# A two-layer hybrid decoder trunk on one core: the gate rows of the attention scores spread over 128 partitions, and another order of work where a residual stage closes

## The reference

```python
c_act = silu(c)
for i in range(2):
    mod = c_act @ ada_w[i] + ada_b[i]
    sh_mix, sc_mix, g_mix, sh_mlp, sc_mlp, g_mlp = split(mod, 6)
    h = rmsnorm(x, norm_mix[i]) * (1 + sc_mix) + sh_mix
    mix = fox_mixer(h) if i == 0 else short_conv_mixer(h)
    x = x + g_mix * mix
    h = rmsnorm(x, norm_mlp[i]) * (1 + sc_mlp) + sh_mlp
    x = x + g_mlp * (square(relu(h @ w_up)) @ w_down)
return rmsnorm(x, final_norm)
```

```python
s = q_t @ k_s * scale + F[t] - F[s]      # s <= t only
```

## Time and profile before

| | before |
|---|---|
| median of 3 runs | 2396.4 us (2382.73 to 2397.29) |
| the profiled execution's own time | 2394.39 us |
| its span, first to last instruction | 2392.7 us |
| mean granted clock of TensorE | 0.979 of full |
| PE busy | 2320.2 us, 97% |
| DVE busy | 1630.4 us, 68% |
| ACT busy | 1052.2 us, 44% |
| transfers | 615.61 MB, mean 257 GB/s |

### The profile page before, as it was taken

How to read it: one execution, slowest core, us unless ns; L and a number is a source line. 1 busy time by engine, 2 the same in 40 slices (tenths; PEclk the granted TensorE clock), 3 DMA queues, 4 the chain that set the end, 5 groups by cost and what they waited for, 6 DMA issues and landing times.

```text
span 2392.7 us, 29047 instructions
## 1 busy us (share of the span) xinstructions
PE 2320.2 (97%) x11331; PEld 1952.3 (82%) x11331; DVE 1630.4 (68%) x1539; ACT 1052.2 (44%) x1183; POOL 173.1 (7%) x338
## 2 busy tenths in 40 slices
PE   5999999989999999999998999998999999999998
PEld 5988989768888888888886888876888888888886
DVE  5757877767866766776776888755786455455455
ACT  4344433445434434434444444444543443443443
POOL 0001111100100100100100111100010000000000
PEclk8999999999999999999998999999999999999999
DMA  9978878767977977987984899854896655655563
GB/s 364 387 247 282 310 275 334 269 245 246 313 274 246 314 277 239 323 281 227 324 282 161 312 339 332 310 164 153 280 320 208 194 189 185 191 192 190 190 201 122
DMA packets 270530, 615.61 MB, mean 257 GB/s; under 512 B 14704, under 2 KB 15040, under 8 KB 269504
## 3 DMA queue, kind: packets, MB, share of 16 engines
q1 hardware_dynamic: 220480, 437.29, 53.9%
q0 software_dynamic: 46080, 167.79, 19.7%
q10 hardware_dynamic: 3840, 8.68, 1.0%
HBM read 611.62 MB, written 2.10 MB: 257 GB/s over the span
## 4 chain that ended last, share of the span: by engine, by line
PE 90%; DMA 3%; DVE 3%; ACT 2%; issue 1%; SPq 0%; ACTq 0%; DVEq 0%
PE ps L441 26%; PE ps L443 26%; PE ps L442 26%; DMA start_ring<-in_ada_w_dram 3%; PE ps L428 2%; PE ps L430 2%; PE ps L429 2%; PE ps L720 1%; PE ps L481 1%; PE ps L478 1%; ACT w_hi L790 1%; DVE acc L1198 1%; DVE w_lo L1183 1%; PE ps L640 0%; PE ps L641 0%
## 5 line engine op out<-in xcount | busy, mean ns | idle before, releaser
L1183 DVE TENSOR_TENSOR w_lo<-raw,w_hi 128x1024 fp32r<-128x1024 f32 x740 | 903.8, 1224 | 624.8 <-ACT w_hi L790 622.5
L790 ACT ACTIVATE w_hi<-raw 128x1024 fp32r<-128x1024 f32 x740 | 783.6, 1060 | 1149.1 <-PE ps L443 1060.7
L441 PE MATMUL ps<-w_hi,h 128*128 128x512 f32 x1536 | 610.1, 397 | 6.5 <-DVE h L1296 6.5
L443 PE MATMUL ps<-w_lo,h 128*128 128x512 f32 x1536 | 602.6, 392 | 0.0
L442 PE MATMUL ps<-w_hi,h 128*128 128x512 f32 x1536 | 602.2, 392 | 0.0
L441 PE MATMUL ps<-w_hi,mid 128*128 128x512 f32 x1280 | 503.7, 393 | 2.6 <-DVE mid L1689 2.6
L443 PE MATMUL ps<-w_lo,mid 128*128 128x512 f32 x1280 | 499.6, 390 | 0.0
L442 PE MATMUL ps<-w_hi,mid 128*128 128x512 f32 x1280 | 499.2, 390 | 0.0
L441 PEld LDWEIGHTS ps<-w_hi,h 128*128 128x128 f32 x1536 | 291.4, 190 | 69.0 <-issue 9.3
L443 PEld LDWEIGHTS ps<-w_lo,h 128*128 128x128 f32 x1536 | 291.0, 189 | 62.1
L442 PEld LDWEIGHTS ps<-w_hi,h 128*128 128x128 f32 x1536 | 291.7, 190 | 59.2 <-issue 0.5
(11 more groups left out here) (201 smaller groups left out, 1248.6 us busy)
## 6 DMA issues: line engine op xcount, KB each, us to landing
ada_raw<-in_ada_w_dram POOLq DMA_DIRECT2D x320, 512.0 KB, 6.3
raw<-in_mlp_w_up_dram SPq DMA_DIRECT2D x128, 1024.0 KB, 5.3
raw<-in_mlp_w_down_dram SPq DMA_DIRECT2D x128, 1024.0 KB, 6.4
raw<-in_fox_w_in_dram SPq DMA_DIRECT2D x48, 1024.0 KB, 9.2
raw<-in_conv_w_in_dram SPq DMA_DIRECT2D x48, 1024.0 KB, 7.2
start_ring<-in_ada_w_dram SPq DMA_DIRECT2D x64, 512.0 KB, 11.7
raw<-in_fox_w_out_dram SPq DMA_DIRECT2D x16, 1024.0 KB, 7.7
raw<-in_conv_w_out_dram SPq DMA_DIRECT2D x16, 1024.0 KB, 5.2
```

Source lines behind the costliest of these rows:

```text
L441: mm(o, xh, hi, start=(k == 0), stop=False)
L443: last = mm(o, xh, lo, start=False, stop=(k == KC - 1))
L790: op(w_hi[:, e % WR], raw[:, e // 2, EK * (e % 2):EK * (e % 2 + 1)], ACT.Copy).then_inc(hi_ready, 1)
L1183: v.tensor_tensor(w_lo[:, e % WR], raw[:, e // 2, EK * (e % 2):EK * (e % 2 + 1)], w_hi[:, e % WR].bitcast(F32), ALU.subtract).then_inc(spl ...
```

## The change

Three things are changed.

1. `sel` and `nf` get 128 partitions. `nf` is cleared once by a new memset on GpSimd (so rows 64 to 127 are zero), the matmul of line 640 reads `sel` [128, 1] broadcast to [128, 128] and `nf` [128, n], and every wait on `const_ready` is raised by one. ACT writes `nf[0:64]` and waits for `const_ready` first.
2. In a closing with a norm (not the last one), `stats_block(norm_i, 0)` runs right after block 0 is added, with `split(un.u, 4)` between the reciprocal and the wait for the root; and `split(un.u, 5)` leaves its place ahead of `add_block(.., 1)`.
3. DVE then makes its chunks of `hb` for pairs 0 and 1 one after the other, then the low part of h's pair 0, then `split(un.u, 5)`, then h's low part of pair 1, then `split` 6 and 7. ACT does `norm_pair` 1 ahead of `split(un.u, 7)`.

```diff
-        sel = sb("sel", [4 * H, H], F32R)
+        sel = sb("sel", [P, H], F32R)
-        nf = sb("nf", [4 * H, T], F32R)
+        nf = sb("nf", [P, T], F32R)
@@ gpsimd
+            pool.memset(nf[:, :].bitcast(F32), 0.0).then_inc(const_ready, 1)
-            pool.wait_ge(const_ready, 7)
+            pool.wait_ge(const_ready, 8)
@@ tensor
-            pe.wait_ge(const_ready, 8)
+            pe.wait_ge(const_ready, 9)
-                    pick = sel[:, NB * g + j:NB * g + j + 1].broadcast_to([4 * H, P])
+                    pick = sel[:, NB * g + j:NB * g + j + 1].broadcast_to([P, P])
@@ scalar
+                act.wait_ge(const_ready, 15)
-                op(nf[:, :], ps[0:4 * H, 7, 0:T], ACT.Copy, scale=-1.0).then_inc(f_act, 1)
+                op(nf[0:4 * H, :], ps[0:4 * H, 7, 0:T], ACT.Copy, scale=-1.0).then_inc(f_act, 1)
...
                 split(un.u, 6)
-                if norm_i is not None:
-                    norm_pair(norm_i, 0)
+                norm_pair(norm_i, 0)
+                norm_pair(norm_i, 1)
                 split(un.u, 7)
-                if norm_i is not None:
-                    norm_pair(norm_i, 1)
-                    scale0(norm_i, 2)
-                    norm_pair(norm_i, 2)
+                scale0(norm_i, 2)
+                norm_pair(norm_i, 2)
@@ vector
-            def inverse_rms(a, calls):
+            def inverse_rms(a, calls, between=None):
                 stat(v.reciprocal(recip[:, a], ms[:, a]))
+                if between is not None:
+                    between()
                 dve.wait_ge(root_ready, calls + 1)
...
+                elif norm_i is not None:
+                    stats_block(norm_i, 0, lambda: split(un.u, 4))
                 else:
                     split(un.u, 4)
-                    if norm_i is not None:
-                        stats_block(norm_i, 0)
                     split(un.u, 5)
                 done(un)
                 add_block(un, n, 1, closed)
...
+                stats_block(norm_i, 1)
+                scale1(norm_i, 0)
+                scale1(norm_i, 1)
+                norm_pair(norm_i, 0, False)
+                norm_pair(norm_i, 1, False)
+                low(norm_i, 0)
+                split(un.u, 5)
+                low(norm_i, 1)
                 split(un.u, 6)
                 split(un.u, 7)
-                if norm_i is not None:
-                    scale1(norm_i, 2)
-                    norm_pair(norm_i, 2)
+                scale1(norm_i, 2)
+                norm_pair(norm_i, 2)
```

More of the change, by code:

```diff
@@ L394, in _ @@
             for i in range(2):
-                pool.wait_ge(const_ready, 9 + i)
+                pool.wait_ge(const_ready, 10 + i)
                 pool.affine_select(out=sel[:, :], in_=sel[:, :].bitcast(F32), compare_op=ALU.not_equal, fill=1.0,
@@ L574, in forget_sums @@
                 pe.wait_ge(f_step, 5)
-                pe.wait_ge(const_ready, 14)
+                pe.wait_ge(const_ready, 15)
                 for a in range(TT):
@@ L1002, in residual @@
                         hooks[i]()
-                if norm_i is not None:
-                    act.wait_ge(added0, r0 // NG + 1)
-                    square(norm_i, n, 0)
+                if norm_i is None:
+                    for i in range(WR, NE):
+                        split(un.u, i)
+                    return
+                act.wait_ge(added0, r0 // NG + 1)
+                square(norm_i, n, 0)
                 if not last:
                     split(un.u, 4)
-                if norm_i is not None:
-                    take_root(norm_i, 0)
-                if norm_i is not None and not last:
+                take_root(norm_i, 0)
+                if not last:
                     scale0(norm_i, 0)
                     scale0(norm_i, 1)
-                if not last:
                     split(un.u, 5)
-                if norm_i is not None:
-                    act.wait_ge(added, r0 + NG)
-                    square(norm_i, n, 1)
-                    take_root(norm_i, 1)
+                act.wait_ge(added, r0 + NG)
+                square(norm_i, n, 1)
+                take_root(norm_i, 1)
                 if last:
@@ L1321, in forget_copy @@
                 dve.wait_ge(f_done, 2)
-                dve.wait_ge(const_ready, 14)
+                dve.wait_ge(const_ready, 15)
                 for c0 in (0, 2 * H):
@@ L1521, in stats_early, with stats_block @@
                 stats[0] += 1
-            def stats_block(i, a):
+            def stats_block(i, a, between=None):
                 dve.wait_ge(squared, TT * NG * i + TT * (NG - 1) + a + 1)
@@ L1526, in stats_block @@
                 stat(v.tensor_scalar(ms[:, a:a + 1], ss[:, a, NG - 1:NG], ss_part[:, a:a + 1], 1.0 / D, ALU.add, ALU.mult))
-                inverse_rms(slice(a, a + 1), TT * i - 1 + a)
+                inverse_rms(slice(a, a + 1), TT * i - 1 + a, between)
             def scale1(i, m):
@@ L1533, in scale1, with norm_pair @@
                 v.tensor_scalar(scratch[:, m % 2, 1, :], xr[:, 1, cols(m)], inv[:, 1:2], None, ALU.mult).then_inc(scaled1, 1)
-            def norm_pair(i, e):
+            def norm_pair(i, e, with_low=True):
                 shift = (0, SH_MLP0, SH_MIX1, SH_MLP1)[i]
@@ L1543, in norm_pair @@
                                 mod[:, KC * shift + k:KC * shift + k + 1], ALU.mult, ALU.add).then_inc(mod_odd, 1)
-                low(i, e)
+                if with_low:
+                    low(i, e)
             def rest_of_norm(i):
@@ L1610, in residual @@
                     return
[L1611 to L1615, removed]
+                if norm_i is None:
+                    split(un.u, 6)
+                    split(un.u, 7)
+                    return
+                stats_block(norm_i, 1)
[6 more added lines that the diff above has]
+                low(norm_i, 1)
                 split(un.u, 6)
-                if norm_i is not None:
-                    norm_pair(norm_i, 1)
                 split(un.u, 7)
-                if norm_i is not None:
-                    scale1(norm_i, 2)
-                    norm_pair(norm_i, 2)
+                scale1(norm_i, 2)
+                norm_pair(norm_i, 2)
             for n in range(NG):
```

## The result

| | before | after |
|---|---|---|
| median of the runs | 2392.7 us (2382.73 to 2397.29, 4 runs) | 2360.84 us (2359.46 to 2361.89, 4 runs) |
| profiled execution | 2394.39 us, span 2392.7 | 2361.78 us, span 2360.1 |
| mean granted clock of the profiled execution | 0.979 | 0.987 |

The ratio of the times is 0.9876, 95% interval 0.9849 to 0.9904: 1.2% faster, and clear of no change.

What follows compares the result with a forecast made beforehand. PE, busy for 97% of the span, sets the end nearly everywhere. Gate rows 25.6 us plus closings 9.9 us take 35.5 from the profiled 2394.4 us, giving 2358.9; with 2.0 for the median, 2361 us, range 2353 to 2368.

Steps and rivals of the forecast that it cites:

- The hold-ups: Score blocks: late weight loads around the 64-partition gate matmul vanish with 128 rows; 4.64 us a block, 17.7 us saved together.
- the rival in which they stay: Score blocks: late weight loads come from something else, so the scores keep their time; 2387 us, chance 0.08.
- The clock behind the blocks: Dense matmuls behind the score blocks: the granted clock stays at 1.00 instead of 0.50, worth 7.9 us.
- The term of 7.9 us: Half of the 15.7 us that dense matmuls behind the four score blocks ran at half clock.
- The closings: Three closings that a norm follows: block 1's square begins earlier, 3.0 + 3.45 + 3.45 = 9.9 us saved, 7 to 11.
- The signs that were named: Closings in the changed profile: PE's `scale1` waits 8 us instead of 18.3; block 1's square starts behind ACT's `w_hi`.
- The new order behind `scale1`, hidden: Behind `scale1` in closings: delayed low parts stay hidden by 1.1 us; if not, under 1 us lost in each closing.
- The base and the total: Whole kernel: 2394.4 us of the profiled execution less 35.5 gives 2358.9; forecast 2361 us, chance 0.62.
- The 2.0 us that I added: Whole kernel: the median of the runs lies 2.0 us above the profiled execution, taking 2358.9 to 2361 us.
- The clock does not fall behind the blocks: Score blocks, rival: the clock falls all the same, leaving a gain of 25.5 us; 2371 us, chance 0.16.
- the closings yield: Closings, rival: another wait replaces the one removed, so only 25.6 us less; 2371 us, chance 0.11.
- the weights don't come late: Weight transfers, rival: landings rise to 20.5 us, PE waits 1 us for each quarter; 2413 us, chance 0.03.

Runs made afterwards that it cites:

- The grouped run: Before with 64 partitions kept, but the eight gate matmuls of a group together at the front of its score block; 2370.5 us, ratio 0.992.
- the clock held: The changed kernel plus 19 matmuls of 512 columns in each closing's gap on PE, 2358.2 us; with the old order behind `scale1` as well, 2360.8 us.

## Why the prediction was right, point by point

- *The hold-ups.* Right, in cause and size. 40 x 0.116 = 4.64 us a block was foretold, 4.5 measured; the rival in which they stay fell. The grouped run adds what the prediction left open: it is the change of the partition count between neighbours.
- *The clock behind the blocks.* Right in the pair of profiled executions: 25.6 us foretold for both together, 4.1 + 7.1 + 7.2 + 7.2 = 25.6 found. As a statement on the median it was too much: 19.8 us. The term of 7.9 us (and the slow parts within the blocks) was read from one execution whose stretches were long.
- *The closings.* 9.9 us foretold; gaps shorter by 3.1, 3.4 and 3.4 us; 9.4 in the medians. ACT ends last ahead of the square, as foretold (1623.85 by its own list, sum ready at 1623.45). The signs that were named were off, though: the waits for `scale1` were to come to 8 us (2.6 in the closing worked out), and came to 10.1 (3.36 there). PE also turns block 0 earlier, by 0.4 us in the first closing and 0.7 in the others, so this part of the gain shows in the wait for `scale0` (1.8 us instead of 3.6), which the prediction left out. The two waits together fall by 10.0.
- *The new order behind `scale1`, hidden.* Right that it costs and brings nothing: the old order with `split` 5 in it takes the same time. The cover was not in the prediction but in that run's expectation, the low clock; with the clock held the old order costs 2.6 us.
- *The base and the total.* 2361 foretold, 2360.84 measured, which is closer than the steps deserve. From the profiled execution's 2394.4 us the steps give 2358.9. Measured is 2361.8 in the like: the start took 1.6 us longer, and from the next unit's start to its last pair it took 25.7, 24.4 and 25.4 us behind the three closings instead of 24.6, 25.5 and 24.4, about 1.2 us more net. All of that is there by pair 1. The first closing shows why: the clock was low equally long in both kernels (529.4 to 539.7 and 504.9 to 515.2), but with the shorter gap 6.0 us of it fall behind the start of the unit, where it was 3.5. In the second closing the stretch itself was 6.8 us instead of 13.7. The prediction allowed for this in its 7 to 11 us. The 2.0 us that I added for the median of three runs happened to make up most of it, which is luck. As a gain, 35.5 us was too much: against before's 31 runs it is 29.2. The level came out because base and terms came from one execution: its long stretches were in the base and were taken away in full.
- *The rivals.* The clock does not fall behind the blocks; the closings yield; the weights don't come late: in the changed kernel quarters of `raw` land after 8.8 us (12 of them from 288 to 380 us), and PE waits for none. The 10.5 us of the earlier trace rows are five transfers late in that window; over all of it nine land after 9.2.

## What to carry to other kernels

A matmul with another partition count among its neighbours can cost more by its two edges than by itself (here 64 among 128): fill its operands with zero rows, or put all such matmuls side by side, and read the starts of the weight loads, not their durations. Where an engine is late by its own list, moving work out of the way is worth the distance to the next that ends, and two waits of the same chain have to be added up before a piece is called worthless. And where a kernel's run time spreads more than its variants', something in it differs from execution to execution: take a term that was read from one execution as a property of that execution until others show it.

## What the runs showed of the hardware

- A weight load next to a change between 64 and 128 partitions starts 0.25 to 0.32 us behind the one before it, otherwise 0.11, whichever count comes first; within eight loads of 64 rows it is 0.11. It is 0.25 to 0.27 where the matmul ahead has 128 columns, and 0.31 to 0.32 where it has 256.
- The granted clock fell from 1.00 to 0.50 in or right behind blocks in which the trace shows no idle time of PE, with eight such matmuls among 40; with four of eight, and with the eight side by side, it stayed at 1.00 in the one profiled run of each. The same blocks had it low for 3.4 to 10.2 us in two profiled executions.
- 19 matmuls of 512 columns with unused results in a gap of 7.5 us held the clock at 1.00, and brought 2.6 us in three gaps. PE stopped once for 1.8 to 2.0 us elsewhere in each kernel that had them.
